# Two residual blocks in split fp32: gate, up, value and embedding-gate products turned to token-major, and every phase begun with its first 128 tokens

## The reference, cut to what matters

```
for i in range(DEPTH):                                   # DEPTH = 2, d_ff = 2816
    g = norm_gains[i]
    f = swiglu_2(rmsnorm_2(h, g[0]), ffn_gate[i, 0], ffn_up[i, 0], ffn_down[i, 0])
    h = h + MACARON * rmsnorm_2(f, g[1])
    mix = hybrid_mixer(rmsnorm_2(h, g[2]), ...)          # latent attention and dilated attention, 8 heads each
    h = h + rmsnorm_2(mix, g[3])
    f = swiglu_2(rmsnorm_2(h, g[4]), ffn_gate[i, 1], ffn_up[i, 1], ffn_down[i, 1])
    h = h + MACARON * rmsnorm_2(f, g[5])
    gate = jax.nn.sigmoid(rmsnorm_2(h, g[6]) @ w_ple_gate[i])
    h = h + rmsnorm_2((p[i] @ w_ple[i]) * gate, g[7])
```

## Time and profile before

| | |
|---|---|
| median of 3 runs | 1837.92 us (1836.95 to 1840.16) |
| the profiled execution's own time | 1842.03 us |
| its span, first to last instruction | 1840.4 us |
| PE, PEld busy | 94%, 87% |
| DVE, ACT, POOL busy | 66%, 49%, 7% |
| mean granted TensorE clock | 0.973 |

### The profile page before, as it was taken

How to read it: one execution, slowest core, us unless ns; L and a number is a source line. 1 busy time by engine, 2 the same in 40 slices (tenths; PEclk the granted TensorE clock), 3 DMA queues, 4 the chain that set the end, 5 groups by cost and what they waited for, 6 DMA issues and landing times.

```text
span 1840.4 us, 29946 instructions
## 1 busy us (share of the span) xinstructions
PE 1734.6 (94%) x11826; PEld 1595.6 (87%) x11826; DVE 1216.6 (66%) x1599; ACT 896.8 (49%) x1235; POOL 122.2 (7%) x163
## 2 busy tenths in 40 slices
PE   6987899999899999999998999988999999999996
PEld 4986799989799998999896899978999896799986
DVE  7889787777765546555676665556655676765556
ACT  4572433356544335434476544345433557644345
POOL 2023111111010000000011000000000003000000
PEclk9998899999999999999999999998999999999999
DMA  9775598868345453555340555434555532355551
GB/s 380 280 292 182 209 358 315 308 232 312 144 172 206 182 183 134 199 193 189 136 178 10 184 200 187 177 138 148 196 193 182 172 138 69 126 184 185 180 197 42
DMA packets 61924, 353.79 MB, mean 192 GB/s; under 512 B 6522, under 2 KB 9738, under 8 KB 27792
## 3 DMA queue, kind: packets, MB, share of 16 engines
q1 hardware_dynamic: 40064, 281.24, 42.2%
q0 software_dynamic: 18384, 66.66, 10.1%
q10 hardware_dynamic: 3392, 4.72, 0.8%
HBM read 349.45 MB, written 3.15 MB: 192 GB/s over the span
## 4 chain that ended last, share of the span: by engine, by line
PE 78%; DVE 11%; ACT 4%; issue 3%; DMA 3%; POOL 0%; DVEq 0%; ACTq 0%; POOLq 0%
PE bank L528 23%; PE bank L529 23%; PE bank L530 23%; DVE w_lo L1509 2%; ACT w_hi L1021 2%; PE bank L560 1%; PE bank L562 1%; PE bank L561 1%; DMA shared<-in_mods 1%; PE bank L700 1%; DVE shared L1530 1%; PE bank L721 1%; DVE shared L2046 1%; PE bank L710 1%; DVE x L2055 1%
## 5 line engine op out<-in xcount | busy, mean ns | idle before, releaser
L528 PE MATMUL bank<-a_hi,w_hi 128*128 128x256 f32 x2648 | 758.8, 287 | 11.0 <-DVE a_lo L1577 3.6
L529 PE MATMUL bank<-a_lo,w_hi 128*128 128x256 f32 x2648 | 754.6, 285 | 0.0
L530 PE MATMUL bank<-a_hi,w_lo 128*128 128x256 f32 x2648 | 754.5, 285 | 0.0
L528 PEld LDWEIGHTS bank<-a_hi,w_hi 128*128 128x128 f32 x2648 | 513.9, 194 | 17.8 <-issue 11.5
L529 PEld LDWEIGHTS bank<-a_lo,w_hi 128*128 128x128 f32 x2648 | 514.0, 194 | 2.9 <-issue 0.7
L530 PEld LDWEIGHTS bank<-a_hi,w_lo 128*128 128x128 f32 x2648 | 513.5, 194 | 0.0
L1771 DVE TENSOR_TENSOR w_lo<-raw,w_hi 128x2048 fp32r<-128x2048 f32 x144 | 330.0, 2292 | 258.2 <-ACT w_hi L1162 258.2
L1162 ACT CAST w_hi<-raw 128x2048 fp32r<-128x2048 f32 x144 | 273.9, 1903 | 268.9 <-PE bank L530 268.9
L1509 DVE TENSOR_TENSOR w_lo<-raw,w_hi 128x2048 fp32r<-128x2048 f32 x119 | 272.1, 2292 | 133.5 <-ACT w_hi L1021 133.4
L1021 ACT CAST w_hi<-raw 128x2048 fp32r<-128x2048 f32 x122 | 231.3, 1907 | 90.9 <-PE bank L530 84.4
L528 PE MATMUL bank<-w_hi,hid_hi 128*128 128x512 f32 x548 | 215.8, 394 | 4.8 <-DVE hid_lo L2192 3.0
(11 more groups left out here) (242 smaller groups left out, 1948.8 us busy)
## 6 DMA issues: line engine op xcount, KB each, us to landing
raw<-in_stream SPq DMA_DIRECT2D x266, 1024.0 KB, 4.8
shared<-in_mods POOLq DMA_DIRECT2D x102, 512.0 KB, 6.3
grow<-in_rows POOLq DMA_DIRECT2D x12, 512.0 KB, 4.0
work<-in_mods POOLq DMA_DIRECT2D x8, 512.0 KB, 9.7
bias_rows<-work ACTq DMA_DIRECT2D x1, 2048.0 KB, 19.0
x<-in_x_t SPq DMA_DIRECT2D x1, 1024.0 KB, 6.2
x<-in_x_d ACTq DMA_DIRECT2D x1, 1024.0 KB, 4.9
work<-bias_rows ACTq DMA_DIRECT2D x1, 1024.0 KB, 10.5
```

The lines of the kernel that those rows point to most:

```text
L528: pe.matmul(out, w_h, v_h, start=start, stop=False, skip_group_check=True)
L529: pe.matmul(out, w_h, v_l, start=False, stop=False, skip_group_check=True)
L530: return pe.matmul(out, w_l, v_h, start=False, stop=stop, skip_group_check=True)
```

## The change

1. **Wide token-major products** (`wide_slab`). A slab of gate and up weights now holds 512 rows of the width by 256 gate and 256 up columns; the second slab of the pair holds the other 512 rows. TensorE holds 128 tokens and streams 512 weight columns: 12 matmuls of 512 for a slab and 128 tokens. The values of the first block's attention, the dilated values and the embedding gates are done so too (two, two and four slabs). In the second block the token norm is now a scalar for each partition, so the row products of DVE and the `mean_row`s of the FFNs fall away; one `mean_row` for each layer is left, after the value slabs.
2. **Transposes of the hidden features** (`turn_hid`). The hidden features come out token-major and are turned by four transposes of 128 by 128 in each group, after the first slab of the next group; ACT and DVE then split them from the bank.
3. **Phases begin with 128 tokens** (`first_tokens`, `token_pair`). Only the two transposed pieces of tokens 0 to 127 stand before the first product; the pieces of the others are turned inside the second quarter of the pair. ACT and DVE norm and split in pieces of 4 chunks by 128 tokens, and the second slab's split (`split_to(b + 2)`) stands between those pieces.
4. **Order.** In the mixer the value slabs come first, the latents and the query and key slabs after them, and `sC` follows the last key slab. In the first block's attention the values come first as well. The embedding product stands between the first and second pair of gate slabs. At the end of FFN 0 the two last `mod` steps stand before the last hidden product, and `mod_reduce(G_KV)` before the last down product. Most `keep_warm`s of the second block are gone.

The core of the diff (indentation shortened by 12):

```diff
+def wide_slab(slot, out, t, k, at=None, between={}):
+    for c in range(4):
+        if at is not None:
+            pe.wait_ge(nl_ready, at + CH * t + 4 * k + c + 1)
+        mm = product(out[:, :], tokens(a_hi, 4 * k + c, t), tokens(a_lo, 4 * k + c, t), *weights(slot, 512 * c, 512),
+                     start=(k == 0 and c == 0), stop=(k == 1 and c == 3))
+        if c in between:
+            between[c]()
     return mm
...
+def turn_piece(src, ready, p):
     t, h = p // 2, p % 2
     pe.wait_ge(*ready(p))
-    if free is not None:
...
-            mm.then_inc(turned, 1)
-def turn_x(u, src, ready):
-    for p in range(4):
-        turn_piece(src, ready, p, (f_ready, 4 * u + 4) if p == 1 else None)
+    for c in range(4):
+        mm = pe.transpose(bank[4 + p][:, c * P:(c + 1) * P], src[:, t, (4 * h + c) * P:(4 * h + c + 1) * P], ident[:, :])
+    mm.then_inc(turned, 1)
+def first_tokens(src, ready, warm=0, b=1):
+    keep_warm(warm, b)
+    for p in range(2):
+        turn_piece(src, ready, p)
+def token_pair(s, outs, at, src, ready):
+    need_slab(s)
+    wide_slab(s, outs[0], 0, 0, at)
+    need_slab(s + 1)
+    wide_slab(s + 1, outs[0], 0, 1, at, {1: lambda: turn_piece(src, ready, 2), 3: lambda: turn_piece(src, ready, 3)}).then_inc(half_done, 1)
+    wide_slab(s, outs[1], 1, 0, at).then_inc(slab_done, 1)
+    wide_slab(s + 1, outs[1], 1, 1, at).then_inc(slab_done, 1)
...
+    def first_half(done, slot, par, free=None):
+        pe.wait_ge(lo_ready, done)
+        if free is not None:
+            pe.wait_ge(hl_ready, free)
+        wide_slab(slot, bank[2 * par], 0, 0)
+        wide_slab(slot, bank[2 * par + 1], 1, 0).then_inc(slab_done, 1)
+    def second_half(done, slot, par):
+        pe.wait_ge(lo_ready, done)
+        wide_slab(slot, bank[2 * par], 0, 1).then_inc(half_done, 1)
+        wide_slab(slot, bank[2 * par + 1], 1, 1).then_inc(slab_done, 1)
+    def turn_hid(par, done):
+        for t in range(2):
+            pe.wait_ge(hid_done, done + (t + 1))
+            for k in range(2):
+                mm = pe.transpose(bank[2 * par][:, k * S + t * P:k * S + (t + 1) * P], hid[:, par, t * S + k * P:t * S + (k + 1) * P], ident[:, :])
+            mm.then_inc(hid_turned, 1)
+    def down(j, done, slot, par, first=False, last=False, pieces=range(4)):
+        pe.wait_ge(lo_ready, done)
         pe.wait_ge(hl_ready, j + (f0 + 1))
-        sums_slab(slot, hid_hi[:, par], hid_lo[:, par], first, last).then_inc(slab_done, 1)
-    pe.wait_ge(lo_ready, b + 2)
-    slab_pair((b, b + 1), (bank[0], bank[2]), before(APPLY_CHUNKS, ap))
-    between()
-    group(None, b + 3, b + 2, None, 1)
+        return sums_slab(slot, hid_hi[:, par], hid_lo[:, par], first, last, pieces)
+    token_pair(b, (bank[0], bank[1]), before(APPLY_CHUNKS, ap), src, ready)
+    if between is not None:
+        between()
+    first_half(b + 3, b + 2, 1)
+    turn_hid(0, 2 * f0)
+    second_half(b + 4, b + 3, 1)
     if i < 2:
         pe.wait_ge(grow_ready, 2 * (2 * i + 2))
-    down(0, b + 5, b + 4, 0, first=True)
+    down(0, b + 5, b + 4, 0, first=True).then_inc(slab_done, 1)
     with pe.Fori(0, (FJ - 3) // 2) as k:
         for h in range(2):
-            group(2 * k + (2 + h), 6 * k + (b + 6 + 3 * h), b + 5 + 3 * h, None, h)
-            down(2 * k + (1 + h), 6 * k + (b + 8 + 3 * h), b + 7 + 3 * h, (1 + h) % 2)
+            first_half(6 * k + (b + 6 + 3 * h), b + 5 + 3 * h, h, 2 * k + (1 + h + f0))
+            turn_hid((1 + h) % 2, 4 * k + (2 * (1 + h) + 2 * f0))
+            second_half(6 * k + (b + 7 + 3 * h), b + 6 + 3 * h, h)
...
-    group(j, b + 3 * j, b + 3 * j - 1, None, j % 2)
-    down(j - 1, b + 3 * j + 2, b + 3 * j + 1, (j - 1) % 2)
-    down(j, b + 3 * j + 3, b + 3 * j + 2, j % 2, last=True)
+    first_half(b + 3 * j, b + 3 * j - 1, 0, j - 1 + f0)
+    turn_hid(1, 2 * (f0 + j - 1))
+    second_half(b + 3 * j + 1, b + 3 * j, 0)
+    down(j - 1, b + 3 * j + 2, b + 3 * j + 1, 1, pieces=(0, 1))
+    turn_hid(0, 2 * (f0 + j))
+    down(j - 1, b + 3 * j + 2, b + 3 * j + 1, 1, pieces=(2, 3)).then_inc(slab_done, 1)
+    if i == 0:
+        mod_reduce(G_KV, 3)
+    down(j, b + 3 * j + 3, b + 3 * j + 2, 0, last=True).then_inc(slab_done, 1)
 def attention(heads, qk, pv, at={}):
...
     b = base2(l, M_MIX)
...
-        need_slab(b + i)
...
+    mean_row(l)
+    for i in range(6):
+        need_slab(b + 2 + i)
+        if i in (2, 3):
+            pe.wait_ge(qkv_act, c0 + i - 1)
+        if i in (4, 5):
             pe.wait_ge(qkv_dve, d0 + i - 3)
-        if i < 6:
-            mm = feature_slab(b + i, bank[i % 4])
-        else:
-            mm = token_slab(b + i, bank[i % 4])
-        mm.then_inc(slab_done, 1)
+        feature_slab(b + 2 + i, bank[i % 4]).then_inc(slab_done, 1)
+        if i == 3:
+            norm_stat(norm2(l, L_QLAT))
         if i == 4:
-            norm_stat(norm2(l, L_QLAT))
-        if i == 5:
             norm_stat(norm2(l, L_KVLAT))
     sC, sQ = b + 8, b + 9
...
     pe.wait_ge(qkv_dve, d0 + 6)
...
-        token_slab(base2(l, M_PGATE) + i, bank[4 + i], None, at if i == 0 else None).then_inc(slab_done, 1)
+    sums_slab(pg + 2, hid_hi[:, 1], hid_lo[:, 1], True, False).then_inc(slab_done, 1)
+    need_slab(pg + 3)
+    for t in range(2):
+        mm = wide_slab(pg + 3, bank[2 * t + 1], t, 0)
+    mm.then_inc(slab_done, 1)
+    need_slab(pg + 4)
+    wide_slab(pg + 4, bank[1], 0, 1).then_inc(half_done, 1)
+    wide_slab(pg + 4, bank[3], 1, 1).then_inc(slab_done, 1)
...
+def turned_hi(u, p, gain):
+    t, h = p // 2, p % 2
+    act.wait_ge(turned, 4 * u + p + 1)
+    for c in range(4 * h, 4 * h + 4):
+        act.activation(tokens(a_hi, c, t), turned_at(c, t), ACT.Copy, scale=gain(c)).then_inc(nh_ready, 1)
...
-        if done is not None:
-            act.wait_ge(slab_done, done)
-        act.copy(hid_hi[:, par].rearrange("p c s -> p (c s)"), hid[:, par, :]).then_inc(hh_ready, 1)
+        for t in range(2):
+            if t == 0:
+                act.wait_ge(half_done, j + (h0 + 1))
+            else:
+                act.wait_ge(slab_done, done)
+            act.activation(gate_s[:, par, t * S:(t + 1) * S], bank[2 * par + t][:, 0:S], ACT.Silu,
+                           scale=pre_r[:, t:t + 1] if i >= 2 else 1.0).then_inc(silu_done, 1)
+    def hidden_hi(j, par):
...
+    warm_up()
+    piece(0)
+    piece(1)
+    split_to(b + 2)
+    piece(2)
+    turned_hi(u, 0, gain)
+    piece(3)
+    for p in range(1, 4):
+        turned_hi(u, p, gain)
+    split_to(b + 3)
 for l in range(LAYERS2):
...
+    act.wait_ge(rpre_ready, 4 * l + 2)
+    act.wait_ge(rows_zero, 4)
+    for t in range(2):
+        if t:
+            act.wait_ge(slab_done, b + 2)
+        else:
+            act.wait_ge(half_done, halves_ffn(3 + 2 * l))
+        act.activation(v_dil[:, t, :], bank[2 + t][:, :], ACT.Copy, scale=pre_r[:, t:t + 1]).then_inc(qkv_act, 1)
+        split_to(b + 4)
+    pre_row_copy(l)
+    split_to(b + 5)
     squares(norm2(l, L_QLAT), lambda c: q_lat[:, c, :], lambda c: act.wait_ge(qkv_dve, d0 + 1))
-    split_to(b + 5)
...
+        split_to(b + min(8 + i, 10))
         if i == 2:
             rsqrt(norm2(l, L_QLAT), 256)
...
+def turned_low(ap, p, gain):
+    at, t, h = before(APPLY_CHUNKS, ap), p // 2, p % 2
+    dve.wait_ge(nh_ready, at + 4 * p + 4)
+    for c in range(4 * h, 4 * h + 4):
+        dve.scalar_tensor_tensor(out=tokens(a_lo, c, t), in0=turned_at(c, t), scalar=gain(c), in1=tokens(a_hi, c, t).bitcast(F32),
+                                 op0=ALU.mult, op1=ALU.subtract).then_inc(nl_ready, 1)
...
+    add(0)
+    add(1)
+    add(2)
+    scaled(0)
+    if last is not None:
+        last()
+    add(3)
+    low(0)
+    split_to(b + 2)
+    scaled(1)
+    for p in range(1, 4):
+        low(p)
+    split_to(b + 3)
...
+    def hidden(j, par):
+        for t in range(2):
+            dve.wait_ge(silu_done, 2 * j + (2 * f0 + t + 1))
+            out, up, gate = hid[:, par, t * S:(t + 1) * S], bank[2 * par + t][:, S:2 * S], gate_s[:, par, t * S:(t + 1) * S]
+            if i >= 2:
+                ins = dve.scalar_tensor_tensor(out=out, in0=up, scalar=pre_r[:, t:t + 1], in1=gate, op0=ALU.mult, op1=ALU.mult)
+            else:
+                ins = dve.tensor_tensor(out, up, gate, ALU.mult)
+            ins.then_inc(hid_done, 1)
...
-    split_to(b + 4)
+    split_to(b + 3)
+    if i >= 2:
+        dve.wait_ge(rpre_ready, v + 1)
+    hidden(0, 0)
     if i < 2:
...
-    gate(0, 0, b + 1, True)
-    hidden(0, 0, b + 2, True)
-    split_to(b + 5)
+    split_to(b + 4)
     angle(0)
...
     j = FJ - 1
-    gate(j, j % 2, b + 3 * j)
-    split_to(b + 3 * j + 3)
-    hidden(j, j % 2, b + 3 * j + 1)
     if i == 0:
         mod(G_A1, 6)
-    split_to(b + 3 * j + 4)
-    hidden_lo(j, j % 2)
-    if i == 0:
         mod(G_A1, 7)
-    split_to(b + 3 * j + 5)
+    hidden(j, 0)
+    split_to(b + 3 * FJ + 1)
+    hidden_lo(j, 0)
...
+    gained(0)
+    gained(1)
+    add(0)
+    gained(2)
+    turned_low(ap, 0, gain)
```

(13 more changed lines are left out.)

657 lines of the change are left out of this document (282 added, 375 removed).

## The result

The changed kernel takes 1848.32 us (median of 14 runs, 1843.87 to 1852.59); the kernel before, in the same set, 1840.38 (14 runs). The ratio is 1.0040, 95% interval 1.0028 to 1.0052: slower by 0.4%, about 8 us. The forecast was 1851. The profiled execution took 1850.60, span 1848.9, mean granted clock 0.973, as before.

What follows compares the result with a forecast made beforehand. TensorE, busy 94% of the span, was taken to bound the kernel, with waiting at phase boundaries. Terms -3.6, -13.6, +16.6, +12.7 and +1 gave +13.1 on 1837.92: 1851 us, range 1822 to 1872.

Steps and rivals of the forecast that it cites:

- loops, with the last groups: FFN groups outside the boundaries: merged matmuls save 0.59 us, transposes cost 0.53, so -0.06 for each of sixty groups: -3.6 us.
- boundaries, eight: Phase starts outside the mixers and FFN 0's end: first products start earlier, most given back; together -13.6 us.
- the two mixers: Mixer starts: TensorE waits for mean_row and the latent chain, and the clock drops; 71.0 us each, together +16.6.
- end of FFN 0: Last group to key-value pair's end: the last turn_hid waits behind mod steps, mod_reduce and clock add: +12.7 us.
- clock elsewhere, and the rest: Clock drops at the other boundaries, where the kernel before has some of its own: +1 us.
- The sign: Whole kernel: slower by more than about 0.2% (3.7 us) was given 0.68, faster by more 0.22, within 0.10.
- the likeliest case: Whole kernel: the forecast itself, 1851 us, own range 1840 to 1864, chance 0.56.
- the two mechanisms that decide the sign: TensorE waits before the latent's products in both mixers (7.5 us each) and before FFN 0's last turn_hid (10.5).
- The 13 ns: TensorE matmuls: overhead above 106.7 and 213.3 ns, paid half as often with 512 columns; saves 0.59 us a group.
- the rule of the Trainium skill: Rival for TensorE loops: each merged pair saves 2.5 ns, not 13, so 33 us less saved: 1884 us, chance 0.02.
- measured in the same way: Four boundaries without own rows: second embedding gate -2.2, a layer's start -1.2, first block's FFN starts -1.2 and -2.1 us.
- a boundary which starts 4 us earlier yields 0.3: Boundary near 1026: first product 4.2 us earlier, but first down product at 30.3 instead of 30.63 us.

Runs made afterwards that it cites:

- e1: Changed kernel with VectorE's two mod pairs for A1 put behind the last group's hidden product and its low part in FFN 0: 1837.47 us, ratio 0.9988.
- e3: Changed kernel with the key latent's norm ahead of the last key slab's rotation in both mixers, query latent's scaling last: 1833.91 us, ratio 0.9969.
- g3: Changed kernel with every product of 512 weight columns issued as two of 256, same order of work otherwise: 1881.42 us, ratio 1.0225.
- e5: Changed kernel with the token-first start undone at every pair, second slab's cast and subtraction ahead of the norm work: 1920.58 us, ratio 1.0439.
- g1: Changed kernel with filler matmuls in the large holes: 40 steps before FFN 0's last turn_hid, 32 before each mixer's latent products: 1842.76 us, ratio 1.0015.
- f1: Changed kernel with the edits of e1, e3 and e4, mod_reduce(G_KV) behind the last down product, mean_row one feature slab later: 1816.98 us, ratio 0.9892.
- e4: Changed kernel with the cast and subtraction for the second FFN group's second half ahead of the first silus and hidden product: 1838.88 us, ratio 0.9998.
- f2: Changed kernel with longer filler: 80 steps before FFN 0's last turn_hid, 60 before each mixer's latent products: 1858.33 us, ratio 1.0108.
- f3: Changed kernel with every transpose of the hidden product done twice, 8 instead of 4 in each of 66 groups: 1867.93 us, ratio 1.0155.

## Why the prediction was right

Step by step, profiled execution against profiled execution (us, change against before):

| step | predicted | measured |
|---|---|---|
| loops, with the last groups | -3.6 | -6.0 |
| boundaries, eight | -13.6 | -13.5 |
| the two mixers | +16.6 | +15.9 |
| end of FFN 0 | +12.7 | +12.8 |
| clock elsewhere, and the rest | +1 | -0.7 |
| sum | +13.1 | +8.5 |

The sign and the likeliest case held, and so did the two mechanisms that decide the sign; e1 and e3 show both by taking them away. The group in the loop (16.81 us), the spacing of 227 ns and both holes are where and as long as the prediction said. The 4.6 us between the sum and the result are sizes. That 1851 lies so near 1848.3 is in part luck: the change was forecast as 13.1 us and is 7.9 by the medians, and the kernel before came out at 1840.38, not at the 1837.92 that I had added it to.

*Loops.* Transposes were taken at 0.53 and cost 0.36 to the next product plus about 0.1 behind it, so a group saves 0.16 and not 0.06. The 13 ns held (g3). The row is not further from its forecast because a second error had the other sign: I multiplied by sixty groups, but two groups of each FFN lie in its boundary and one in the end of FFN 0. 53 groups are left, with 58 sets of transposes. By my own prices that is 53 times -0.59 and 58 times +0.53, -0.5 us and not -3.6; with the 0.43 that a set cost it is -6.3. By the rule of the Trainium skill (TensorE: Matmul & The Clock Gate, "Wait — 56ns, not 53.3ns?") a merged pair would have saved 2.5 ns; the measured 12.3 decide against it for matmuls that each bring their own weights. FFN 1 stands in this row with 0.5 lost instead of 1.0 saved, from the lower clock behind the hole below.

*Boundaries.* The sum is right by luck in part. Near 1026 the inner times were close: first product at +2.8 (2.9), second quarter 6.6 (6.9), third 11.0 (11.5), pair end 16.5 (16.95). But the silu chain was oversized, a hole of 1.1 us where I had 2.0, so that boundary gave -1.4 and not -0.3; the FFN of the last layer -3.5 (-2.4), the start of the second layer -3.4 (-1.2). FFN 0's start gave -1.0 (-1.2). On the other side FFN 1's start gave nothing, +0.4 (-2.1). The step that failed at FFN 1 is "measured in the same way": I did not follow FFN 1's VectorE queue. The positions land at 535.1, the chain of small operations behind them ends at 538.5, a subtraction and then `hidden_lo(0)` follow, and TensorE, early now, waits 3.3 us; 13 matmuls at the lower level come on top (in the row above). The other boundaries: out of the first block -0.5 (-1.3), the embedding gates -2.3 and -1.9 (-2.9, -2.2).

I wrote that a boundary which starts 4 us earlier yields 0.3. As a difference to the kernel before it was 1.4. As a statement on the token-first start it was too low: in e5 this boundary is 6 us longer without it, where the norm work is still cut by tokens and what this start covers is lost. That is an upper bound, as e5 moves the second slab too.

*Mixers.* `mean_row` waited 1.9 us, the latent hole was 7.5 (7.5 predicted), and the clock cost 2.4 by the first score (2.5). By g1's stretches it is 1.3 and 2.7, and with the same hole the time from it to the next boundary was 74.3 to 76.5 us over the variants that leave it alone, by how long the lower level lasted.

*End of FFN 0.* The hole was 9.7 us (10.5), the last hidden product at +24.3 after the group's start (24.6), the pair ended 20.5 after the last down product (20.0). e1 and g1 split it: about 8 for the wait, 2 for the clock. Of `mod_reduce`, 3.5 in the sum, moving it back won 0.3 in f1, since the filler and the transposes then stand behind it; its cost on the path was real, but no cheaper place was found.

*Clock elsewhere.* I charged 1 for drops at the other boundaries. They are there, but no worse than before: two boundaries that stood at 0.91 and 0.90 are at 0.95 and 1.00 after, and the first block's exit is at 0.95 in both. The rest of that row is small differences in the attention stretches and the start.

## What to carry to other kernels

When TensorE's work is cut or moved, look at what the moved piece covered: value slabs had hidden a norm chain of 11 us, and VectorE's filler steps stood ahead of a product that nobody had waited for. Both were worth more than the matmul saving, and both could be read from the queues of the kernel before. Then repair the order of the slower engines and measure again, before the change is judged: the same products went from 0.4% slower to 1.4% faster. Follow every boundary's queue, not one and its likes.

## What the runs showed of the hardware

- A hole can cost more than its length, and equal holes do not cost the same. After 3.3 us of it (start of FFN 1) 13 matmuls of 512 columns ran at 427 ns before the spacing was 227 again, 2.7 us more; in e3 the same place has a hole of 3.15 us and the down product behind it runs at the full rate (24 matmuls start within 5.33 us). After 2.5 us (e3) the next 12 of 256 columns took 2.70 us in the first mixer and 1.51 in the second. Where the filler of g1 ran until 0.4 us before them they took 1.53 in both.
- The clock also varies where a kernel is unchanged. The stretch from the first embedding gate to the second mixer was 233.4 us in both profiled executions of the changed kernel and 230.7 in five of its variants (e1, e3, e4, f2, g1), four of which have no edit there; the granted clock is 0.99 in the changed kernel and 1.00 in e1. Where no lower level falls into a stretch, unedited stretches agree within 0.05 us (191.87 to 191.91 us for the FFN after the first mixer in six profiled executions). The start of the kernel, up to the first transpose, took 191.8 to 197.2 us. Reading an edit from its own stretch, at the same granted clock, avoids taking this for a gain (e4: 5 us its own, 8 by the medians; f3: 26 its own, 18 by the medians).
- A filler step written as one full-precision matmul of 128 columns is two in the trace, 0.111 us each.
